# Expert token gather: always 128 offsets, expert block first, and neighbouring slots four partitions apart

## The reference

```python
lg = uf @ w_rg + b_rg                                   # (264, 4): group
_, gsel = lax.top_k(lg, 1)
le_sel = jnp.take_along_axis(le, gsel[:, :, None], axis=1)[:, 0]
v2, i2 = lax.top_k(le_sel, TOP_K_EXPERT)                # 2 experts of the group's 8
gate = g1 * jax.nn.softmax(v2, axis=-1)
...
h = jax.nn.silu(jnp.einsum('td,edf->tef', u, w_gate)) * jnp.einsum('td,edf->tef', u, w_up)
h = h * comb[:, :, None]
return jnp.einsum('tef,efd->td', h, w_down)             # 32 experts, 2048 x 256 each, x3, float32
```

## Time and profile before

| | |
|---|---|
| time, three runs | 1571.71 us median (1568.71 to 1578.26) |
| profiled execution, own time | 1566.98 us, span 1565.2 us |
| PE busy | 1274.4 us (81%) |
| DVE busy | 672.5 us (43%) |
| POOL busy | 61.8 us (4%) |
| DMA, mean rate | 368 GB/s over the span, 576.64 MB |
| pairs of experts | 16 |
| indirect DMAs on xg, on y_rows | 16, 32 |

### The profile page before, as it was taken

One profiled execution on the slowest core, in us unless ns is written; L12 is line 12 of the kernel. 1 busy time (PEld: TensorE's weight loads), 2 busy tenths in 40 slices (PEclk: granted clock), 3 DMA queues, 4 the chain that ended last, 5 costly groups with the idle time before them and its releaser, 6 DMA issues. The chain is left out here.

```text
span 1565.2 us, 24701 instructions
## 1 busy us (share of the span) xinstructions
PE 1274.4 (81%) x7862; PEld 806.4 (52%) x7863; DVE 672.5 (43%) x4782; ACT 229.8 (15%) x453; POOL 61.8 (4%) x107
## 2 busy tenths in 40 slices
PE   7999788889889798847999977788787778678783
PEld 5777455556556466424667533544444444344451
DVE  4536855757657576758664671121000001000004
ACT  2121002212122122111020111011000010100011
POOL 1000000000000000001000000001000000100000
PEclk9999999999899899867999996789899998888996
DMA  9767999999999999999999899989999999999974
GB/s 310 269 205 292 389 389 394 384 392 375 375 400 378 382 396 372 410 402 374 374 403 402 330 410 367 422 346 415 399 421 382 390 389 371 369 387 386 376 338 172
DMA packets 173996, 576.64 MB, mean 368 GB/s; under 512 B 18457, under 2 KB 78666, under 8 KB 160058
## 3 DMA queue, kind: packets, MB, share of 16 engines
q1 hardware_dynamic: 145616, 541.70, 89.6%
q10 hardware_dynamic: 23842, 24.68, 4.6%
q0 software_dynamic: 4432, 9.05, 1.8%
HBM read 568.74 MB, written 17.77 MB: 375 GB/s over the span
## 5 line engine op out<-in xcount | busy, mean ns | idle before, releaser
L128 DVE CUSTOM_DVE_ANT_0 ws<-ws,xgT 128x128 f32<-128x128 f32 x1792 | 388.1, 284 | 200.9 <-DMA ws<-in_cache_fox_k 173.0
L1931 PE MATMUL bank<-ws,xgT 128*64 128x256 f32 x1024 | 261.0, 420 | 103.7 <-DMA ws<-in_w_expert_up 99.4
L982 PE MATMUL bank<-xn,ws 128*128 128x264 f32 x1152 | 291.0, 408 | 7.9 <-DMA ws<-in_w_in 7.9
L982 PEld LDWEIGHTS bank<-xn,ws 128*128 128x128 f32 x1152 | 223.8, 200 | 109.3 <-issue 55.5
L1933 PE MATMUL bank<-ws,xgT 128*64 128x256 f32 x1024 | 261.1, 420 | 0.0
L1931 PEld LDWEIGHTS bank<-ws,xgT 128*64 128x64 f32 x1024 | 152.9, 152 | 209.4 <-DMA ws<-in_w_expert_up 110.2
L967 PE MATMUL bank<-ws,PR 128*32 128x512 f32 x1024 | 149.2, 663 | 80.5 <-DMA ws<-in_cache_fox_v 76.2
L2131 DVE COPY gu<-bank 128x256 f32<-128x256 f32 x32 | 13.6, 425 | 386.9 <-PE bank L1933 386.9
L1933 PEld LDWEIGHTS bank<-ws,xgT 128*64 128x64 f32 x1024 | 152.8, 152 | 0.0
L128 DVE DVE_READ_ACCUMULATOR2_ANT Z<- 128x1 f32 x1792 | 142.1, 79 | 0.0
L1953 PE MATMUL bank<-ws,hT 128*32 128x512 f32 x1024 | 116.1, 606 | 12.3 <-ACT xgT L2030 12.1
(11 more groups left out here) (439 smaller groups left out, 979.0 us busy)
## 6 DMA issues: line engine op xcount, KB each, us to landing
ws<-in_cache_sb_k SPq DMA_DIRECT2D x128, 512.0 KB, 8.3
ws<-in_cache_fox_k SPq DMA_DIRECT2D x128, 512.0 KB, 12.9
ws<-in_cache_sb_v SPq DMA_DIRECT2D x128, 512.0 KB, 8.9
ws<-in_cache_fox_v SPq DMA_DIRECT2D x128, 512.0 KB, 12.7
ws<-in_w_expert_gate SPq DMA_DIRECT2D x32, 2048.0 KB, 21.9
ws<-in_w_expert_up SPq DMA_DIRECT2D x32, 2048.0 KB, 26.4
ws<-in_w_expert_down SPq DMA_DIRECT2D x32, 2048.0 KB, 25.4
ws<-in_w_in SPq DMA_DIRECT2D x24, 2048.0 KB, 21.3
```

Of the source, the lines that this page charges most:

```text
L128: ins = dve.tensor_tensor_reduce(k, k, qb[:, (g * H + h) * HD:(g * H + h + 1) * HD], 1.0, 0.0, ALU.mult, ALU.add, Z[:, n % 2, g, h, t:t + 1])
L982: mm = pe.matmul(out[:, 0:T], w[:, c, m * P:(m + 1) * P], xn[:, c, :], start=(c == 0), stop=(c == KC - 1))
L1931: pe.matmul(bank[2 * k][0:SLOTS, 0:256], lhs, ws[:, wg, c * 256:(c + 1) * 256], start=(c == 0), stop=(c == KC - 1))
```

## The change

`slot_of` and the transposes' output pattern change together: partition p = 32 b + 4 l + s now belongs to slot 32 b + 8 s + l, with b from 0 to 3, l from 0 to 7, s from 0 to 3. The block (expert) is now the outermost part, so partitions 0 to 63 are the first expert and 64 to 127 the second, and slots that follow each other lie four partitions apart. The flag `many2`, its reduction on DVE and POOL's branch go; each gather takes all 128 offsets. The scatters, the weights' loads and all matmuls but the transposes are as they were.

```diff
-            own.step(pool.iota(io32[:, :].rearrange("p (h b s) -> p h b s", h=2, b=2), [[HALF, 2], [SLOTS, 2], [1, HALF]],
+            own.step(pool.iota(io32[:, :].rearrange("p (b l s) -> p b l s", b=4, l=8), [[HALF, 4], [1, 8], [8, 4]],
                                base=0, channel_multiplier=0))
...
-                        out = bank[4 + k][:, c * P:(c + 1) * P].rearrange("p (b h s) -> p h b s", b=2, h=2)
+                        out = bank[4 + k][:, c * P:(c + 1) * P].rearrange("p (b s l) -> p b l s", b=4, l=8)
                         mm = pe.transpose(out, xv[:, 4 * k + c, :], ident[:, :])
...
-                red(many2[:, :], manyf[0:1, :].rearrange("p (n b) -> p n b", b=2), ALU.max)
...
-            def gather(n, rows):
-                pool.indirect_dma_start(xg[0:rows, :], None, u_rows[0:SEQ, :],
-                                        bass.IndirectOffsetOnAxis(ap=idx[0:rows, n:n + 1], axis=0),
+            def tokens(n):
+
+                wait_past(pool, E["xgp"], 4 * n)
+                pool.indirect_dma_start(xg[:, :], None, u_rows[0:SEQ, :],
+                                        bass.IndirectOffsetOnAxis(ap=idx[:, n:n + 1], axis=0),
                                         bounds_check=SEQ - 1, oob_is_err=False).then_inc(E["xg"], 16)
-
-            def tokens(n):
-
-                rest = pool.value_load(many2[0:1, n:n + 1], min_val=0, max_val=1)
-                wait_past(pool, E["xgp"], 4 * n)
-                with pool.If(rest > 0):
-                    gather(n, P)
-                with pool.Else():
-                    gather(n, SLOTS)
```

More of the change, by code:

```diff
@@ L219, in hybrid_step @@
         many = sb("many", [1, BLOCKS], I32)
-        many2 = sb("many2", [1, PAIRS], I32)
         iota = sb("iota", [P, P])
@@ L689, in hybrid_step @@
                             cTs, FB, ptr, ws, W, kring, vring, qb, Z, key_caches, value_caches, w_in, bank, S, C, E, wr, br, xg, xgT, idx, dest,
-                            gates, extra, many, many2, iota, destc, drow, xs_pc, g_pc, sqs, srs, outs, u_rows, start, A,
+                            gates, extra, many, iota, destc, drow, xs_pc, g_pc, sqs, srs, outs, u_rows, start, A,
                             osum, blk, PR, zs, zr, sp_h, run, ts, zx)
@@ L696, in hybrid_step @@
         experts(nc, ctx, ws, W, a, ident, ones, iota, gcol, lastq, xT, xn, xgT, xg, wr, br, bank, sem, E, idx, dest, gates, extra,
-                many, many2, destc, drow, sqs, srs, y_prompt, y_sample, u_rows, y_rows)
+                many, destc, drow, sqs, srs, y_prompt, y_sample, u_rows, y_rows)
 STEPS = NB * PAGES
@@ L1764, in experts @@
 def experts(nc, ctx, ws, W, a, ident, ones, iota, gcol, lastq, xT, xn, xgT, xg, wr, br, bank, sem, E, idx, dest, gates, extra,
-            many, many2, destc, drow, sqs, srs, y_prompt, y_sample, u_rows, y_rows):
+            many, destc, drow, sqs, srs, y_prompt, y_sample, u_rows, y_rows):
     def sb(name, shape, dt=F32, where=ctx):
```

## The result

| | before | changed |
|---|---|---|
| time, median of four runs | 1570.21 us (1567.69 to 1578.26) | 1527.71 us (1525.46 to 1529.98) |
| ratio | | 0.9721, 95% interval 0.9682 to 0.9760 |
| profiled execution | 1566.98 us | 1527.54 us |

The change makes the kernel faster by 2.8%.

The account below looks back on a forecast made before the run. The prediction took weight traffic, slowed by 64-offset gathers, to bound the experts' stage. Twelve periods falling from 34.28 to 31.67 us (31.3) plus 1.1 ahead gave 32.4 us off the 1571.71 median: 1539 us, range 1528 to 1558.

Parts of the forecast that it names:

- The bound and the place: Experts' stage: held by weight traffic; TensorE starts each pair's second expert when the second up weight has landed.
- Slow stretches go: While 64-offset gathers move: traffic slowed to about 250 GB/s recovers, 2.4 us a gather, 24 us over ten periods.
- It is the 64-offset form: Gathers in the experts' stage: the 64-offset form slows everything beside it, not its bytes; 255 and 247 against 423 GB/s.
- What a gather costs instead: Each new pair period: 0.85 us over the 30.82 without a gather, so 31.67; twelve periods save 31.3 us.
- 1.1 us ahead of the first period: Gather at 1062.6, before the first second-up-weight arrival: its slow stretch goes, saving 1.1 us.
- The sum: Whole kernel: 32.4 us saved, 1534.6 from the profiled execution, 1539.3 against the median; forecast 1539.
- The low end, 1528: Whole kernel: lower end of the forecast range 1528 to 1558 us, with about 0.15 chance outside the range.
- a gather for nothing: Best case in the 12 periods: gathers cost nothing, 12 × 3.46 + 1.1 = 42.6 us saved, 1529 us.
- Rival 1: Pair periods: offsets help, the spread doesn't; period 32.2, 1546 us, or at full gather cost 33.5, 1562; chance 0.17.
- Rival 2: Gather stretches: no gain, the slowdown belongs to something other than the 64 offsets; 1571 us; chance 0.07.
- Rival 3: Transposes: strided PSUM writes make them TensorE's bound; slower from 4.8 times as long, 1668 us at eight times; chance 0.04.

Follow-up runs that it names:

- table of six orders: Six kernels, one without gathers, the others differing in slot order or offsets: 0 to 72 rows on the busiest engine in nine gathers; nine periods take 276.93 to 297.97 us.
- offsets alone: Kernel before with every gather taking 128 offsets, old order of the slots kept: 1552.16 us, ratio 0.9888.
- spacing alone: Kernel before, 64 offsets and branch kept, with neighbouring slots four partitions apart inside the 64: 1549.99 us, ratio 0.9880.

## Why the prediction was right in its mechanism, and where it was off

- **The bound and the place: right.** The stage was held by the second up weight before and still is; the changed kernel's chain and waits show it, as the kernel without gathers does.
- **Slow stretches go: right, in size too.** Forecast 24 us; the packets lost 23.6 before and 0.3 after.
- **"It is the 64-offset form", its bytes have no part in it: half right.** Without rows the form costs nothing (1524.54), with half of the rows about half, and by placing them otherwise it costs two thirds. It is the form together with the rows.
- **What a gather costs instead, 0.85 us: too high.** (377.12/12) − 30.82 = 0.61 us, the lower bound of the bytes alone, 0.62. I took a value between the two ends and this step cost 12 × 0.24 = 2.9 us of the miss. By the count behind the table of six orders, the nine gathers put two or three rows each on the busiest engine, 23 in all. That the engines nearly even this out within a pair is a reading of these numbers; no run isolates it.
- **1.1 us ahead of the first period: the term that failed.** It came out as 6.5. It was worked out from one gather's slow stretch, that of the fourth pair, and it left out the first two gathers, which take 128 offsets in both kernels but whose rows the new order moves as well. Three things lie in the 6.5 us.
  - The program reaches the first gather 1.2 us earlier (947.6 to 946.4, rows below). That is not the change: the second trace of the changed kernel reaches it at 943.2.
  - The first gather is on the path itself. Its rows move in 3.6 us before and in 1.3 after, TensorE waits for its landing, 6.5 us before and 4.4 after, and the first weights matmul starts 51.55 us behind the gather before and 49.05 after. In the four traces with all of these rows in the old order it is 49.7 to 51.8 us, in the five with the new order 46.9 to 49.3. The prediction had nothing for this.
  - From there the first arrival comes 2.8 us sooner, of which 1.1 was forecast. The rows of the gathers that move in this stretch account for it: with 64 offsets and no rows the stretch is 72.3 us, as in the changed kernel (72.2), where the kernel before has 75.0. But it is 74.6 without gathers, where TensorE was busy 67.5 us in it instead of 65.1, at a granted clock of 0.87 instead of 0.89, so it moves by 2 us by itself too.
- **How loose this part is.** The first arrival lies between 1062.8 and 1075.6 in all kernels that keep the chain, and the two traces of the changed one alone differ by 4.9 us. The forecast had no term for such scatter.
- **Behind the last arrival** the changed kernel lost 1.5 us, for which no step was written. The cause is open.
- **The sum.** On the profiled executions 32.4 was forecast and 39.4 measured: 3.0 more in the 12 periods, 5.4 ahead of them, 0.2 in the last, −1.5 behind. The other 4.5 us of the miss are no step of the mechanism. The profiled execution before was 4.7 us below its median and I added this back, from 1534.6 to 1539.3; the changed kernel's was at its median (1527.54 and 1527.71). Of these, 1.5 us came from the median before, which fell from 1571.71 to 1570.21 with a fourth run.
- **The low end, 1528: too tight.** It was built from "a gather for nothing", 1529, which bounds only the 12 periods. A gather that cost nothing at all gave 1521.19. The end should have had the spread of the rest of the program in it, some 5 us either way. By how little the time missed it is chance: the second set of runs of the same kernel has its median 1.2 us inside.
- **Rival 1 (the spread doesn't help): false, and priced too low in its common case.** A gather in the old order costs 2.33 us, not 1.35, and the spread earns 20.0 us of the 34.3. The attribution in the text, slowdown first and spread as a correction, would have misled anyone who kept only one half: offsets alone give 1552.16, spacing alone 1549.99, both 1527.71. The offsets remove 23 us of slow packets and give about 9 back. That they do so because 128 offsets put the old order's rows on fewer engines fits the rows that move at once in those ten gathers (5 to 7 before, 2 to 6 with offsets only), but no run isolates it.
- **Rival 2 (no gain): false.** The run with offsets only has no slow stretch.
- **Rival 3 (strided PSUM writes): false.** 277 ns each on both sides, over all 240. The Trainium skill's sentence on non-contiguous PSUM access ("SBUF — State Buffer", Door 1) is not borne out for these fp32 transposes with single columns eight apart: the price is 0, where the rival needed a factor of 4.8.

The first gathers and the first wait for their data on TensorE, before and then changed (engine, duration ns min/median/max, first and last start; and the group of the transposes that wait):

```profile
L952 POOL DMA_INDIRECT xg<-u_rows,idx x2: 995/1066/1138, 947.6 to 960.8; - x2
```

```profile
L1155 PE MATMUL bank<-ident,xg 128*128 128x128 f32 x16 | 3.7, 421 | 6.5 <-DMA xg<-u_rows,idx 6.5
```

```profile
L951 POOL DMA_INDIRECT xg<-u_rows,idx x2: 1002/1060/1117, 946.4 to 957.7; - x2
L1922 PE MATMUL bank<-ws,xgT x1024: 379/379/690, 995.4 to 1483.9; 128*64 128x256 f32 x171
```

```profile
L1154 PE MATMUL bank<-ident,xg 128*128 128x128 f32 x16 | 3.7, 422 | 4.4 <-DMA xg<-u_rows,idx 4.4
```

## What to carry to other kernels

When one stream keeps all DMA engines busy, a small transfer beside it costs what its busiest engine carries, not what its bytes come to: count rows by engine for each transfer by itself, since here an engine did not catch up in later transfers (384.41 us against 377.12 when the load was even only in sum). Look at the rate, not only at the busy share: engines that are busy at 250 GB/s where they carry 423 elsewhere name a transfer whose form is wrong. And when a range is built from the best case of one stage, add what the other stages vary by.

## What the runs showed that was not expected

- An indirect gather with 64 offsets makes the packets beside it slow (a loss of 2.4 us a gather), one with 112 does so nearly as much (2.2), one with 128 hardly at all (0.5 us over ten gathers in the old order, 0.3 in the new one), for the same rows.
- The same gather costs 0.66 us or 2.33 us with all 128 offsets, by nothing but the partitions of its rows.
- Evening the load out over the whole stage, at the price of less even single gathers, made it worse (384.41 against 377.12 us).
- In the scatters 128 offsets cost 16.8 us where 64 do well.
